# Modulation products in fp32 on quarters of the array's columns, a reordered front, and the attention mask added by TensorE

## What is computed

```python
def modulation(cond, w, b):
    m = jax.nn.silu(cond) @ w + b
    return [t[:, None, :] for t in jnp.split(m, MOD_CHUNKS, axis=-1)]

def adaln_layer(x, cond, mod_w, mod_b, norm_g, w1, w2, mixer):
    sh1, sc1, gt1, sh2, sc2, gt2 = modulation(cond, mod_w, mod_b)
    h = rms_norm(x, norm_g[0]) * (1 + sc1) + sh1
    mix, aux = mixer(h)
    x = x + gt1 * rms_norm(mix, norm_g[1])
    h = rms_norm(x, norm_g[2]) * (1 + sc2) + sh2
    x = x + gt2 * rms_norm(sq_relu_mlp(h, w1, w2), norm_g[3])
    return x, aux

    # in latent_attention, blocks of 128 queries, 8 heads, keys of three blocks and a cache
    valid = (jnp.abs(kpos - qpos) <= WINDOW) & (kpos >= 0) & (kpos < n)
    s_loc = jnp.einsum('bnqhgd,bnkhd->bnhgqk', qb, kb, preferred_element_type=jnp.float32) * scale
    s_loc = jnp.where(valid[None, :, None, None], s_loc, NEG_INF)
```

## Time and profile before

| what | value |
|---|---|
| median of 3 runs (lowest, highest) | 3009.15 us (3004.49, 3010.03) |
| profiled execution | 3008.46 us, its span 3006.7 us |
| PE busy | 2848.0 us (95%) |
| DVE busy | 1604.5 us (53%) |
| ACT busy | 1365.1 us (45%) |
| DMA | 355.12 MB, mean 118 GB/s |

### The profile page before, as it was taken

How to read it: one execution, slowest core, us unless ns; L and a number is a source line. 1 busy time by engine, 2 the same in 40 slices (tenths; PEclk the granted TensorE clock), 3 DMA queues, 4 the chain that set the end, 5 groups by cost and what they waited for, 6 DMA issues and landing times. The chain is left out here.

```text
span 3006.7 us, 39547 instructions
## 1 busy us (share of the span) xinstructions
PE 2848.0 (95%) x14994; PEld 2472.5 (82%) x14994; DVE 1604.5 (53%) x2409; ACT 1365.1 (45%) x2157; POOL 159.6 (5%) x260
## 2 busy tenths in 40 slices
PE   5999999899999999999999997877999999999998
PEld 3767888679999999999888776766789999999997
DVE  6467777554545444554322456875554554445444
ACT  6445665544444433443322665654444343334333
POOL 0000000000000000000000007840000000000000
PEclk8999999999999999999999998889999999999999
DMA  6443322533334444444313441014333444444443
GB/s 246 147 150 98 99 77 86 154 112 120 125 120 147 126 126 126 147 124 128 93 49 106 133 126 42 1 56 160 103 115 120 126 132 141 126 126 147 126 126 112
DMA packets 309734, 355.12 MB, mean 118 GB/s; under 512 B 20086, under 2 KB 242748, under 8 KB 308572
## 3 DMA queue, kind: packets, MB, share of 16 engines
q1 hardware_dynamic: 300560, 331.52, 35.4%
q10 hardware_dynamic: 7020, 13.87, 1.3%
q0 software_dynamic: 2016, 7.86, 0.7%
HBM read 337.88 MB, written 15.34 MB: 117 GB/s over the span
## 5 line engine op out<-in xcount | busy, mean ns | idle before, releaser
L1259 DVE TENSOR_TENSOR p_lo<-p_raw,p_hi 128x1024 fp32r<-128x1024 f32 x507 | 619.6, 1223 | 695.5 <-ACT p_hi L724 695.2
L724 ACT ACTIVATE p_hi<-p_raw 128x1024 fp32r<-128x1024 f32 x507 | 533.0, 1052 | 567.7 <-DMA p_raw<-mlp_w 421.5
L2023 PE MATMUL ps<-hm_hi,p_hi 128*128 128x384 f32 x1536 | 516.4, 336 | 4.8 <-DVE hm_lo L1279 4.0
L2023 PE MATMUL ps<-hm_hi,p_lo 128*128 128x384 f32 x1536 | 516.4, 336 | 0.0
L2023 PE MATMUL ps<-hm_lo,p_hi 128*128 128x384 f32 x1536 | 515.2, 335 | 0.0
L1962 PE MATMUL ps<-p_hi,hid_hi 128*128 128x512 f32 x1152 | 362.5, 395 | 3.5 <-DVE p_lo L1259 3.5
L1962 PE MATMUL ps<-p_lo,hid_hi 128*128 128x512 f32 x1152 | 357.2, 391 | 0.0
L1962 PE MATMUL ps<-p_hi,hid_lo 128*128 128x512 f32 x1152 | 356.5, 391 | 0.0
L939 ACT ACTIVATE relu<-ps 128x384 f32<-128x384 f32 x192 | 94.5, 492 | 524.8 <-PE ps L2023 524.8
L1496 DVE TENSOR_TENSOR sqr<-relu 128x384 f32<-128x384 f32 x192 | 107.2, 558 | 375.5 <-ACT relu L939 375.5
L2023 PEld LDWEIGHTS ps<-hm_hi,p_hi 128*128 128x128 f32 x1536 | 288.9, 188 | 14.1 <-DVE hm_lo L1279 4.5
(11 more groups left out here) (238 smaller groups left out, 4018.9 us busy)
## 6 DMA issues: line engine op xcount, KB each, us to landing
p_raw<-mlp_w SPq DMA_DIRECT2D x384, 512.0 KB, 3.9
mod_p<-mod_w SPq DMA_DIRECT2D x80, 512.0 KB, 4.1
p_raw<-gla_w_in SPq DMA_DIRECT2D x56, 512.0 KB, 3.6
p_raw<-gla_w_out SPq DMA_DIRECT2D x24, 512.0 KB, 3.3
mod_w<-mod_w SPq DMA_DIRECT2D x8, 1024.0 KB, 13.1
p_raw<-ab_w_in SPq DMA_DIRECT2D x14, 512.0 KB, 5.2
p_raw<-ab_w_out SPq DMA_DIRECT2D x12, 512.0 KB, 3.7
p_raw<-ab_w_out SPq DMA_DIRECT2D x24, 256.0 KB, 3.9
```

The source lines that it names most:

```text
L724: nc.scalar.activation(p_hi[s][:, :, 0:width], p_raw[s][:, :, 0:width], ACT.Copy).then_inc(pan_hi, 1)
L1259: V.tensor_tensor(p_lo[s][:, :, 0:width], p_raw[s][:, :, 0:width], p_hi[s][:, :, 0:width].bitcast(F32), ALU.subtract).then_inc(pan_lo, 1)
L2023: mm = M.matmul(ps[:, b, 0:GN], w[s][:, c, :], x[:, c, :], start=(c == 0 and x is hi and w is p_hi), stop=(c == DC - 1 and w is p_lo))
```

## The change

The first modulation and the 80 late steps are no longer split. The conditioning stands in the array as `csil`, fp32, 32 columns of which 2 are used, the rest zero. Each weight piece is multiplied in four products whose outputs lie on partitions 0, 32, 64 and 96, so that each uses its own quarter of the array's columns: 512 columns each for the first kinds, 256 each for a late step, which now is 128 rows by 1024 columns. `late_hi`, `late_lo`, `csr` and the splits are gone; a round is 8 steps, and there are 10 rounds instead of 20, each turned by two transposes of 128 by 128. There are five buffers of `mod_p` instead of four.

The front is reordered: the conditioning and `ident` come first on SP's queue, x is interleaved with `mod_w`, the tables of the rotation and of attention move from ACT's queue to SP's. ACT squares all of x before it touches h, the ring has four banks, PE turns chunks inside the first three units and waits chunk by chunk, and ACT writes the high part itself for two of eight chunks in groups 1 and 2.

The mask: `band_r` and `ident_r` are fp32r copies, and behind each piece of scores over the outer key blocks PE adds `ident_r` times the mask, 256 or 128 columns for each head; DVE's additions are gone.

```diff
-MODS = 4
-MOD_HI = 2
+MODS = 5
+MOD_ROWS = 32
@@ scalar
-            def turn_take(bank, g, layer, kind, c):
+            def turn_take(bank, g, layer, kind, c, hi=None):
...
+                for out in ([h32[n % 2][:]] if hi is None else [h32[n % 2][:], hi]):
+                    for lo, up, cond in conds(g):
...
-            def late_hi(k):
-
-                act.wait_ge(modp_landed[k % MODS], 16 * (k // MODS + 1))
-                if k >= MOD_HI:
-                    act.wait_ge(modp_used, FIRST_USED + k - MOD_HI + 1)
-                nc.scalar.activation(mod_ph[k % MOD_HI][:], mod_p[k % MODS][:], ACT.Copy).then_inc(mod_hi, 1)
-
@@ vector
-            def late_lo(k):
-
-                dve.wait_ge(mod_hi, FIRST_LO + k + 1)
-                V.tensor_tensor(mod_pl[k % MODS][:], mod_p[k % MODS][:], mod_ph[k % MOD_HI][:].bitcast(F32),
-                                ALU.subtract).then_inc(mod_lo, 1)
-
...
                 for u in range(2):
-                    last = None
-                    for i, tile in enumerate(own_tiles(b)):
-                        if b and tile != b:
-                            cols = s_bank(u)[:, (i + 2) * P:(i + 3) * P]
-                            last = V.tensor_tensor(cols, cols, band[:, tile - b + 1, :], ALU.add)
-                    if last is not None:
-                        own(last)
                     own(V.tensor_reduce(x[:, 0, u:u + 1], s_bank(u)[:, 0:n], AX_X, ALU.max))
@@ tensor
                 for c in range(DC):
+                    if p == 0:
+                        pe.wait_ge(h_ready, DC * n + c + 1)
...
             def late_mod(k):
 
-                q = k // 4
-                if k % 4 == 0 and q:
+                q, b = divmod(k, DC)
+                if b == 0 and q:
                     pe.wait_ge(mod_rows, q + 1)
-                pe.wait_ge(mod_lo, FIRST_LO + k + 1)
-                for w in (mod_ph[k % MOD_HI], mod_pl[k % MODS]):
-                    for a in range(2):
-                        last = M.matmul(ps[0:4, ROWS_BANK, :], csr[:, 2 * (k % 4) + a, :], w[:, a, :],
-                                        start=(k % 4 == 0 and a == 0 and w is mod_ph[k % MOD_HI]),
-                                        stop=(k % 4 == 3 and a == 1 and w is mod_pl[k % MODS]))
+                pe.wait_ge(modp_landed[k % MODS], 16 * (k // MODS + 1))
+                for j in range(4):
+                    last = M.matmul(ps[32 * j:32 * j + MOD_ROWS, ROWS_BANK, 0:256], csil[:, b, :],
+                                    mod_p[k % MODS][:, 256 * j:256 * (j + 1)], start=(b == 0), stop=(b == DC - 1))
                 last.then_inc(modp_used, 1)
...
                         last = M.matmul(s_bank(u)[:, c0:c0 + m * P], q_t[rows, j, b * P:(b + 1) * P], keys, start=True,
-                                        stop=True)
+                                        stop=(b == 0 or first is None))
+                    if b and first is not None:
+                        for u in range(2):
+                            mask = band_r[:, first - b + 1:first - b + 1 + m, :].rearrange("p t n -> p (t n)")
+                            last = M.matmul(s_bank(u)[:, c0:c0 + m * P], ident_r[:], mask, start=False, stop=True)
                 last.then_inc(s_ready, 1)
...
-            for g in range(2):
-                for c in range(DC):
-                    first_turn(g, c)
-            unit(0, lambda c: first_turn(2, c))
+            pe.wait_ge(csil_ready, 1)
+            for b in range(DC):
+                if b == 3:
+                    pe.wait_ge(const_in, 16 * N_CONST)
+                    turn(ps[:, 7, 0:96], rows1[0:96, :])
+                    turn(ps[:, 7, P:P + 86], rows2[0:86, :]).then_inc(vec_turned, 1)
+                if b == 6:
+                    pe.wait_ge(vec_copied, 2)
+                    for c in range(RING):
+                        turn_ahead()
+                pe.wait_ge(mod_landed[b], 16)
+                for j in range(4):
+                    last = M.matmul(ps[32 * j:32 * j + MOD_ROWS, ROWS_BANK, :], csil[:, b, :],
+                                    mod_w[b][:, 512 * j:512 * (j + 1)], start=(b == 0), stop=(b == DC - 1))
+                last.then_inc(modp_used, 1)
```

More of the change, by code:

```diff
@@ L383, in rows_after @@
         def rows_after(u):
-            return [q for q in range(LATE // 4) if mod_unit[4 * q + 3] + 1 == u]
+            return [q for q in range(ROUNDS) if mod_unit[DC * q + DC - 1] + 1 == u]
         def rope_after(u):
@@ L418, in flat, with act_makes_hi @@
             return w[:, :, :].rearrange("p c n -> p (c n)")
+        def act_makes_hi(g, c):
+            return g > 0 and c % 3 == 2
         def conds(g):
@@ L426, in _ @@
             T = Tally()
-            first = io["mod_w"][0][:, 0:2 * D].rearrange("(b p) n -> b p n", p=P)
-            for b in range(DC):
-                sp.dma_start(mod_w[b][:], first[b]).then_inc(mod_landed[b], 16)
+            sp.dma_start(rows3[0:DC, :], io["c_ctx"].rearrange("(r n) -> r n", n=P)).then_inc(cond_in, 16)
+            sp.dma_start(rows3[DC:2 * DC, :], io["c"].rearrange("b (r n) -> (b r) n", n=P)).then_inc(cond_in, 16)
+            sp.dma_start(ident[:], io["c_ident"]).then_inc(cond_in, 16)
             sp.sem_inc(pan_used, SLOTS - 1)
@@ L1348, in conv @@
                 cols = slice(GN * n, GN * (n + 1))
-                w = [vec1[:, 112 + CC * a + i:113 + CC * a + i] for a in range(3)]
+                w = [vec2[:, 74 + CC * a + i:75 + CC * a + i] for a in range(3)]
                 if part == 1:
@@ L1409, in _ @@
                     normalise(pair)
-                for k in mods_after(u):
-                    late_lo(k)
                 if rope_after(u) is not None:
@@ L1824, in late_turn @@
                     pe.wait_ge(ao_taken, outputs[0])
-                for f in range(4):
-                    last = turn(ps[:, TURN_BANK, 4 * f:4 * f + 4], mod_r[:, f * P:(f + 1) * P])
+                for i in range(2):
+                    last = turn(ps[:, TURN_BANK, i * P:(i + 1) * P], mod_r[:, i * P:(i + 1) * P])
                 last.then_inc(mod_turned, 1)
@@ L1877, in output @@
                         v = v_c[:, x, cols] if what == "ctx" else v_n[:, x, cols]
-                        last = M.matmul(ps[cols, O_BANK, P:2 * P], v, weights(p)[1][u][:, i, :], start=(i == 0),
+                        last = M.matmul(ps[cols, O_BANK, 2 * P:3 * P], v, weights(p)[1][u][:, i, :], start=(i == 0),
                                         stop=(i == len(values) - 1))
@@ L1881, in output, with turn_ahead @@
                 outputs[0] = p + 1
-            for g in range(2):
-                for c in range(DC):
-                    first_turn(g, c)
-            unit(0, lambda c: first_turn(2, c))
+            ahead = [(g, c) for g in range(GROUPS) for c in range(DC)]
+            def turn_ahead():
+                if ahead:
+                    first_turn(*ahead.pop(0))
+            pe.wait_ge(csil_ready, 1)
[13 more added lines that the diff above has]
+                last.then_inc(modp_used, 1)
+            pe.wait_ge(mod_rows, 1)
+            for i in range(4):
+                last = turn(ps[:, TURN_MODS, i * P:(i + 1) * P], mod_a[:, i * P:(i + 1) * P])
+            last.then_inc(mod_turned, 1)
+            for u in range(GROUPS):
+                unit(u, lambda c: turn_ahead())
             for u in range(UNITS):
```

244 lines of the change are left out of this document (111 added, 133 removed).

## The result

The median of four runs is 2973.8 us (2971.2 to 2974.5) against 3008.6 us for the kernel before (four runs, 3004.5 to 3010.0): a ratio of 0.9885, 95% interval 0.9868 to 0.9902. That is 35 us less, 7 us short of the forecast's 2967 and inside its range. The profiled execution took 2973.88 us, its span is 2971.8.

The account below looks back on a forecast made before the run. PE was taken as the bound, busy 2848.0 of 3006.7 us. Gains of 18.2 (front), 19.9 (units 3 to 17) and 3.3 (attention), 41.4 in all, gave 2967 us, range 2957 to 2997.

Parts of the forecast that it names:

- the mechanism of the quarters: Late modulation steps: four fp32 products on four column quarters run together, so a step costs 0.43 us; chance 0.70.
- the forecast's second rival: Late steps: quarters run one after another, a step costs 1.73 us, the time is 3072; chance 0.04.
- the masks: Attention units: 112 added mask products on PE and 24 extra mode trips cost 17.0 us.
- The estimate by the Trainium skill's factor of 3.07: Late steps: four small products packed by rows gain 3.07x, so a step would cost 0.56 us, the time 8 us more.
- The forecast's first rival: Late steps: quarters run only two at a time, a step costs 0.87 us, the time is 2995; chance 0.14.
- Units 3 to 17: Units before attention: cheaper bursts 12.5, turning of rows 2.4, less PE idle 5; together 19.9 us gained.
- Attention units: Attention stage: late steps, waits and turned rows give 20.3, masks take 17.0; 3.3 us gained, bounds 8 and -2.
- the extra trip into the row-split mode: Attention, 24 pairs with scores in two pieces around a mask: one more trip at 0.2 us, 4.8 in all.
- The forecast's other step there: Attention: the 112 additions taken off DVE shorten a chain already covered by the next unit's 5 us, gaining nothing.
- Front: Start to end of unit 2: earlier first take 7.9 us, then 24 chunks in 24.2 instead of 34.6; 18.2 us gained.
- ACT's high parts: Front, second and third group: ACT makes 4 of 16 high parts, taking the pace from 0.89 to 0.79 us a chunk.
- The rival of a low clock in the front: Front: clock stays at 1.2 GHz, 24 chunks cost 38 us, front gives 3 instead of 18, time 2982; chance 0.06.

Follow-up runs that it names:

- h: Changed kernel with the four products of each late step sent to one quarter of the array's columns; front's products stay on quarters: 3064.6 us, one run.
- e: Changed kernel with late steps moved: two behind every attention unit, eight behind units 14 to 17, none behind 2 to 13: 2970.0 us.
- a: Changed kernel with the mask added by DVE again instead of by products on PE: 2950.5 us.
- c: Changed kernel with all pieces of the scores first and the mask products behind them: 2963.3 us.
- b: Kernel before with only the mask moved to PE as in the change: 3029.7 us, ratio 1.0069.
- f: Changed kernel with idle products on PE in the front while it waits for weights, ACT's copy and the first chunk: 2974.2 us.
- i_all: Changed kernel with DVE masks, DVE high parts, two late steps behind each attention unit, eight behind units 6 to 9, idle front products: 2939.5 us.
- d: Changed kernel with DVE writing every high part of h, ACT none: 2972.6 us.

## Why the prediction came out as it did

**Right: the mechanism of the quarters, and the size of a step.** A step, eight records in two rounds of four, costs 2 x 0.216 = 0.43 us. h shows the other end, 3.57 for a burst where the forecast's second rival said 3.46 to 3.66. Its 3064.6 us lie near that rival's 3072, or near 3065 without the 7 us by which that rival also had the front worse, since h keeps the front on quarters; the masks (22.4, not 17) and the front (14.1, not 18.2) are in it with errors of their own, so the nearness is partly chance. The estimate by the Trainium skill's factor of 3.07 ("TensorE: Matmul & The Clock Gate", Part 3), 0.56 a step, is not borne out inside a burst, where the factor is 4; a burst of two with its changes of mode, 3.79/1.22, comes to 3.1, close to it. The forecast's first rival took the program order that the Trainium skill states in the same part, and supposed that the two halves of one product stand side by side. The order is not at odds with the trace, where the four records of a round start 6 to 7 ns one after another; the supposition is: on one quarter (h) records start 0.216 us apart, so the four of a round belong to four products.

**Units 3 to 17: -22.7 instead of -19.9,** by errors of both signs. A burst stands for 1.00 us, and the unit behind it takes 4.39 instead of the 4.17 of a bare one (e), so it costs 5.39 - 4.17 = 1.22, not 1.07, against 6.02 - 4.17 = 1.85 before; so the bursts gave 16 x 0.63 = 10.1 and not 12.5. But the idle time fell by 6.4 us, not 5, and its consequence was left out altogether: behind the longest wait the kernel before runs at the lower clock. PE of the kernel before, ten products of one unit:

```profile
113.39 0.52 PE L1736 MATMUL ps<-ident,v_t 128*128 128x128 f32 x3 [2.30 <-ACT v_n L852]
...
115.17 0.52 PE L1795 MATMUL ps<-h_hi,p_hi 128*128 128x384 f32 x1
115.49 0.52 PE L1795 MATMUL ps<-h_lo,p_hi 128*128 128x384 f32 x1
...
118.45 0.33 PE L1795 MATMUL ps<-h_hi,p_hi 128*128 128x384 f32 x1
118.62 0.33 PE L1795 MATMUL ps<-h_lo,p_hi 128*128 128x384 f32 x1
```

1.1 us after the end of 2.30 us of idle the starts of ten products lie 0.32 us apart, then 0.17 again, and the granted clock of 113.6 to 119.0 us is 0.68: 1.5 us lost behind a wait of 2.3. With the wait this is gone too. The turns of rows gave 2.8 us (seven of 0.43 to 0.59 became one of 0.37 and two of 0.17) instead of 2.4. That makes 20.8. Of the other 1.9 us about 1.0 lies in the three bursts of the kernel before that waited for DVE's low part: each cost 0.3 more than a burst in the same place without a wait, besides the wait itself. The last 0.9 isn't placed.

**Attention units: +3.0 instead of -3.3.** The gains were right as a sum, 19.4 us (a) against 20.3. The masks cost 22.4 against 17.0, and the term that failed is the extra trip into the row-split mode, put at 0.2 us from one product that followed such a mode, and 0.40 by c (9.6 instead of 4.8 us). The products were right, 12.8 us against 12.2. The result lies outside this stage's bounds: -2 was the worst it allowed, and its upper bound of 8 should be 10 by its own terms (3.3 + 1.9 + 4.8). The forecast's other step there, that DVE's additions had been covered and taking them off DVE gains next to nothing, is confirmed by a and b: it is a change that buys idle time on an engine that is not the bound, with work on the one that is.

**Front: -14.1 instead of -18.2,** in three pieces. The last quartet started at 39.17, not 37.5 (1.7): the rate from 3 us on was the 0.39 MB/us assumed, which gives 38 for 13.6 MB, but 14.1 MB had moved by then, so transfers queued behind the weights had run beside the last of them. From there to the first take it is 4.24, not 3.8 (0.4; the forecast's own terms add up to 3.6): that is the half clock, for at the full one it is 2.91 (f). From the first take to the end of unit 2 it is 26.3, not 24.2 (2.1). Here i_all, at the full clock and with all high parts by DVE, needs 24.8; ACT's high parts add 0.8 (f against i_all) and the half clock 0.6 (the changed kernel against f), and the first 0.6 is not split further. ACT's high parts were to bring the pace from 0.89 to 0.79, and it went to 0.96: DVE waits about 0.5 us for each high part that ACT writes, and ACT then waits 0.2 to 0.5 us for DVE, which the forecast had not reckoned; d removes it.

The rival of a low clock in the front was thus partly true: PE, which waits for DMA there, fell to half at 38.3 us and was back at 48.6 in this execution (back at 51.5 in e, and at 35.8 in c, ahead of the last quartet), never through all 24 chunks. No run takes the front's two changes apart, the queue's new order and the weights that are no longer split; how the 14.1 us divide between them is open.

**The total** is 7 us above the forecast, inside the forecast's own range of 2957 to 2980. The stages are off by 4.1 and 6.3 us to the bad side and by 2.8 to the good, and the part behind attention took 1.2 us less by its own spread, so the nearness of the total is partly luck.

## What to carry to other kernels

Small fp32 products with few output rows are worth placing on different quarters of the array's columns, where they ran four at a time here (0.43 us for four against 1.73) and needed no splitting by ACT and DVE. Before moving work to the engine that bounds the kernel, ask what it frees: here the moved mask cost 22 us and bought only idle time on DVE. Where a cheap filler (a late step) can stand anywhere, put it where the bounding engine waits for another, and when moving it away look at which waits it had covered.

## What the runs showed of the hardware

- Changing from products on 64 rows to full ones and back once more within a pair costs 0.40 us (c), about twice what the longer first product behind such a change suggests. It sits in four places of 0.1 each, by the distances between starts in the changed kernel. From scores to mask: 314.308 - 314.002 = 0.31 where scores follow each other in 0.21, and from the first mask to the next product 0.22 where it is 0.12 behind another mask (c). Back again: 0.21 from the second mask to the scores instead of 0.12, and 0.21 from the first pair of 128 columns to the next instead of 0.11 (c).
- Four fp32 products of 256 columns take 0.43 us on four quarters and 1.73 on one (h): the factor is the full four.
- A wait of 2.3 us in the kernel before was followed by 3.2 us at the lower clock, so it cost 3.8 us in all; behind the waits of 1.70 us there and of 2.00 us in e the products kept their 0.17. In the front PE's records show half pace (1.93 us a quartet) from 16 to about 31 us although the granted clock of that stretch reads 1.00. The trace's record of the clock begins at 31.5 us (25.6 in the kernel before, where the distance of two products falls from 0.43 to 0.23), and the views read 1.00 where there is no record; from there on clock and pace agree.
- The first group of chunks, the same in all changed kernels, took 8.0 to 9.4 us from one execution to the next, by when the clock fell and rose (7.97 in c, 9.41 in e).
